# Raw weights and low parts in one buffer, seven weight homes, and a token tile at a time at the layer's seams

## The reference, cut to what matters

```python
h = layer_norm(x, ln_in_g, ln_in_b)
for i in range(DEPTH):                                   # DEPTH = 2, alpha = DN_ALPHA
    q, k, v, xr, yr, ga, gr = split(h @ w_in[i])         # 1024, 256, 256, then four of 1024 columns
    attn = local_attention(rope(q), rope(k), v, sink[i]) # 8 heads, window 128
    hr = rg_lru(conv(xr), forward) + rg_lru(conv(xr), backward)   # gates: two matmuls, then a scan
    rnn = hr * gelu(yr)
    merged = sigmoid(ga) * (attn @ w_proj_attn[i]) + sigmoid(gr) * (rnn @ w_proj_rnn[i])
    h = layer_norm(alpha * h + merged @ w_out[i], ln1_g[i], ln1_b[i])
    gate, val = split(h @ w_up[i])                       # 3072 columns each
    ffn = (gelu(conv3(gate)) * val) @ w_down[i]
    ple = sigmoid(h @ w_ple_gate[i]) * (p[i] @ w_ple[i])
    h = layer_norm(alpha * h + ffn + ple, ln2_g[i], ln2_b[i])
return h
```

## Time and profile before

| | us |
|---|---|
| median of 3 runs (985.03 to 986.15) | 985.28 |
| span of the profiled execution, first to last instruction | 984.2 |
| what lies around the span, by the median | about 1.1 |
| PE busy | 942.2 |
| DVE busy | 727.9 |
| ACT busy | 576.5 |
| DMA engines, mean share of the span | about a half |

### The profile page before, as it was taken

The page is one execution under the profiler, slowest core; times in us unless marked ns, Lnnn a source line. Parts: engine busy times, 40 slices in busy tenths (PEclk is TensorE's granted clock), DMA queues, the critical chain, the costliest instruction groups (busy, mean ns, idle before and its releaser), DMA issues.

```text
span 984.2 us, 12616 instructions
## 1 busy us (share of the span) xinstructions
PE 942.2 (96%) x5056; PEld 804.8 (82%) x5056; DVE 727.9 (74%) x974; ACT 576.5 (59%) x724; POOL 1.4 (0%) x9
## 2 busy tenths in 40 slices
PE   4999999999899999999979999999998999999995
PEld 2998889888678888888769888898886888888884
DVE  6879886777758676667777889877676776676658
ACT  3589988643356555546246999984335565455550
POOL 0000000000000000000000000000000000000000
PEclk9999999999999999999989999999999999999998
DMA  9464436384355656554725454455733755556541
GB/s 313 129 207 164 166 109 213 129 281 160 134 196 177 208 164 204 188 188 157 267 65 189 156 192 153 149 170 182 246 129 131 251 175 192 193 177 204 175 171 43
DMA packets 117753, 174.62 MB, mean 177 GB/s; under 512 B 3904, under 2 KB 78400, under 8 KB 117056
## 3 DMA queue, kind: packets, MB, share of 16 engines
q1 hardware_dynamic: 117408, 173.27, 52.6%
q10 hardware_dynamic: 288, 0.56, 0.1%
HBM read 172.76 MB, written 1.05 MB: 177 GB/s over the span
## 4 chain that ended last, share of the span: by engine, by line
PE 79%; DVE 14%; ACT 5%; issue 2%; DMA 1%; SPq 0%; DVEq 0%; ACTq 0%
PE ring L538 18%; PE ring L489 12%; PE ring L491 12%; PE ring L490 12%; PE ring L540 9%; DVE sb_w_lo L1089 4%; PE misc L489 4%; PE misc L491 4%; PE misc L490 4%; ACT sb_w_hi L787 2%; PE misc L637 2%; DVE sb_h L1139 1%; PE misc L695 1%; DVE sb_h L1136 1%; PE misc L675 1%
## 5 line engine op out<-in xcount | busy, mean ns | idle before, releaser
L1089 DVE TENSOR_TENSOR sb_w_lo<-sb_raw,sb_w_hi 128x2048 fp32r<-128x2048 f32 (+1 forms) x168 | 363.1, 2163 | 156.9 <-ACT sb_w_hi L787 156.6
L787 ACT CAST sb_w_hi<-sb_raw 128x2048 fp32r<-128x2048 f32 (+1 forms) x168 | 303.0, 1806 | 116.8 <-PE ring L491 73.6
L538 PE MATMUL ring<-sb_x_both,sb_w_hi 128*128 128x512 f32 x768 | 271.1, 398 | 3.3 <-DVE sb_w_lo L1089 3.3
L540 PE MATMUL ring<-sb_x_both,sb_w_lo 128*128 128x256 f32 x768 | 215.2, 280 | 0.0
L538 PEld LDWEIGHTS ring<-sb_x_both,sb_w_hi 128*128 128x128 f32 x768 | 144.2, 188 | 39.6 <-DVE sb_w_lo L1089 4.2
L489 PE MATMUL ring<-sb_w_hi,sb_x_both 128*128 128x512 f32 x352 | 142.5, 405 | 6.2 <-DVE sb_w_lo L1089 4.3
L540 PEld LDWEIGHTS ring<-sb_x_both,sb_w_lo 128*128 128x128 f32 x768 | 144.9, 189 | 0.3
L490 PE MATMUL ring<-sb_w_lo,sb_x_both 128*128 128x512 f32 x352 | 138.8, 394 | 0.0
L491 PE MATMUL ring<-sb_w_hi,sb_x_both 128*128 128x512 f32 x352 | 138.7, 394 | 0.0
L489 PEld LDWEIGHTS ring<-sb_w_hi,sb_x_both 128*128 128x128 f32 x352 | 67.3, 191 | 23.3 <-issue 4.4
L491 PEld LDWEIGHTS ring<-sb_w_hi,sb_x_both 128*128 128x128 f32 x352 | 67.0, 190 | 14.6
(11 more groups left out here) (140 smaller groups left out, 1335.1 us busy)
## 6 DMA issues: line engine op xcount, KB each, us to landing
sb_raw<-in_w_up_dram SPq DMA_DIRECT2D x48, 1024.0 KB, 5.2
sb_raw<-in_w_in_dram SPq DMA_DIRECT2D x44, 1024.0 KB, 5.2
sb_raw<-in_w_down_dram SPq DMA_DIRECT2D x24, 1024.0 KB, 5.0
sb_raw<-in_w_proj_attn_dram SPq DMA_DIRECT2D x8, 1024.0 KB, 5.0
sb_raw<-in_w_proj_rnn_dram SPq DMA_DIRECT2D x8, 1024.0 KB, 5.1
sb_raw<-in_w_out_dram SPq DMA_DIRECT2D x8, 1024.0 KB, 5.1
sb_raw<-in_w_ple_gate_dram SPq DMA_DIRECT2D x8, 1024.0 KB, 5.0
sb_lnp<-in_ln_dram SPq DMA_DIRECT2D x5, 1024.0 KB, 7.2
```

What stands on the lines that cost most here:

```text
L538: nc.tensor.matmul(bank_of(*key), w_hi[:, slot, cols], x_both[:, k], start=k == 0, stop=False)
L540: last = nc.tensor.matmul(bank_of(*key)[:, 0:SEQ], w_lo[:, slot, cols], x_hi[:, k], start=False, stop=k == KT - 1)
L787: nc.scalar.copy(w_hi[:, W_OF[n], 0:size], raw[:, slot, 0:size]).then_inc(s_hi_part, 1)
L1089: nc.vector.tensor_tensor(w_lo[:, W_OF[n], 0:size], raw[:, RAW_OF[n], 0:size], hi, ALU.subtract).then_inc(s_split, 1)
```

## The change

The source line numbers of the new kernel differ (cast L822, low part L1128, load L454, transposes L654, L1186 the add of the down product).

- **Homes.** `raw` and `w_lo` are now one buffer: DVE subtracts in place. There are five such homes with their `w_hi`, and two more that borrow other tensors while these are idle: `hb` with the scan's tensors (from `wo0` to the next layer's `q1`), and `r_lo`/`r_hi` (from `pg0` to the next layer's `q1`). A load now waits until PE has finished with the home's former item, since that item's low part lies there; the cast waits for the load alone. Homes go to the item in order of last use. `AHEAD` is 3, in places 4 or 5.
- **Output seam.** `wo0` and `wo1` run together, tile 0 through both, then tile 1, with the turns of tile 0 between the matmuls of tile 1; `pg0` tile 0, ple with the turns of tile 1, `pg0` tile 1. `pg1` follows here and no longer ahead of `d4`.
- **Layer seam.** `d4` and `d5` run together by tile; the first half of the next layer's tile 0 is turned inside tile 1 of `d5`; `q0` tile 0, one turn, a part of `q1` tile 0, the other turn, `q0` tile 1. `q1` moves from the second place in the mixer to here.
- **Mixer.** `WITH_BLOCK` loses `q1` and takes in `yr1`, and its order changes, so attention starts a block earlier. `yr0` is copied first and gets its gelu later.
- **Down products on DVE.** `add_ffn` adds the down product and takes the statistics half a tile at a time, and the high and low parts of `x_parts` go in between.
- **Embedding.** The two 128x2048 operations on DVE stand in groups j = 1 and j = 2 of the up units. `p_in` is loaded later, into `tmp`.

The core of the diff:

```diff
-BY_TILE = ("q0", "wo1", "pg0", f"d{LAST}")
-
-WITH_BLOCK = ("xr1", "q1", "kv", "ga0", "ga1", "gr0", "gr1", "yr0")
...
+WITH_BLOCK = ("xr1", "kv", "ga0", "ga1", "yr0", "gr0", "gr1", "yr1")
+
+
+def items_of():
+
+    items = [("q0", 0), ("q0", 1), ("q1", 0), ("q1", 1), ("xr0", 0), ("xr0", 1)]
+    for i, name in enumerate(WITH_BLOCK):
+        items += [(name, 0), (f"rg{i // RNN_BLOCKS}", i % RNN_BLOCKS), (name, 1)]
+    items += [(name, part) for name in ("pa0", "pa1", "pr0", "pr1") for part in range(2)]
+    items += [("wo0", 0), ("wo1", 0), ("wo0", 1), ("wo1", 1), ("pg0", 0), ("pg0", 1), ("ple", 0), ("ple", 1),
+              ("pg1", 0), ("pg1", 1)]
+    for j in range(FF_GROUPS):
+        names = [f"g{j}", f"v{j}"] + ([f"d{j - 1}"] if 0 < j < LAST else [])
+        items += [(name, part) for name in names for part in range(2)]
+    return items + [(f"d{j}", part) for j in (LAST - 1, LAST) for part in range(2)]
+
+
+ITEMS = [(l, name, part) for l in range(DEPTH) for name, part in items_of()]
 ITEM = {item: n for n, item in enumerate(ITEMS)}
-W_SLOTS = 3
-RAW_SLOTS = 3
-AHEAD = 2
+W_SLOTS = 5
+STATE_HOME, RNN_HOME = W_SLOTS, W_SLOTS + 1
+HOMES = W_SLOTS + 2
+AHEAD = 3
...
+def homes_of(n):
+
+    l, name, part = ITEMS[n]
+    at = n - ITEM[l, "q0", 0]
+    start, first, second = (ITEM[l, key, 0] - ITEM[l, "q0", 0] for key in ("xr0", "wo0", "pg0"))
+    homes = list(range(W_SLOTS))
+    if at < start or at >= first:
+        homes.append(STATE_HOME)
+    if at < start or at >= second:
+        homes.append(RNN_HOME)
+    return homes
+
+
+HOME, FORMER, LOADED = [], [], []
+_latest, _loads = {}, [0] * HOMES
+for _n, (_l, _name, _part) in enumerate(ITEMS):
+    _home = min(homes_of(_n), key=lambda home: _latest.get(home, home - HOMES))
+    _former = _latest.get(_home)
+    if _home >= W_SLOTS and _n > ITEM[_l, "xr0", 0] and (_former is None or _former < ITEM[_l, "xr0", 0]):
+        _former = "state" if _home == STATE_HOME else "rnn"
+    FORMER.append(_former)
+    HOME.append(_home)
+    _latest[_home] = _n
+    _loads[_home] += 16 * item_loads(_n)
+    LOADED.append(_loads[_home])
...
+        w_lo, at = sb_at("w_lo", [P, W_SLOTS, 2048], F32R)
+        raw = again("raw", [P, W_SLOTS, 2048], F32, at)
...
+        raw_at = [raw[:, i] for i in range(W_SLOTS)] + [whole(hb[:, :, :]), r_raw[:, :]]
+        hi_at = [w_hi[:, i] for i in range(W_SLOTS)] + [scan_hi[:, :], whole(r_hi[:, :, :])]
+        lo_at = [w_lo[:, i] for i in range(W_SLOTS)] + [hb_lo[:, :], whole(r_lo[:, :, :])]
...
+                former = FORMER[n]
+                if former == "state":
+                    sp.wait_ge(s_rnn_ready, value("rnn_ready", ITEMS[n][0], 2))
+                elif former == "rnn":
+                    sp.wait_ge(s_products, PRODUCT[ITEMS[n][0], "pr1", 1])
+                elif former is not None:
+                    sp.wait_ge(s_products, last_product(former))
+                home = HOME[n]
...
                 load_norm(l, 1)
-                for n in range(ITEM[l, "wo0", 1], ITEM[l, f"d{LAST}", 1] + 1):
+                sp.dma_start(p_in, a["p"][bass.ds(l, 1), 0].rearrange("a (t q) c -> q (a t) c", q=P)
+                             ).then_inc(s_p, 16)
+                for n in range(ITEM[l, "wo0", 0], ITEM[l, f"d{LAST}", 1] + 1):
...
+            def last_down_units(l):
+
                 for t in range(TT):
+                    for hh in range(2):
+                        if t == 0:
+                            pe.wait_ge(s_f_ready, value("f_ready", l, 2 * (LAST - 1) + hh + 1))
+                        part = down_part(l, LAST - 1, hh, t)
+                        if t == 1:
+                            part.then_inc(s_products, 1)
+                    if t == 1 and l + 1 < DEPTH:
+                        turn_h(l + 1, 0, 0, [0])
                     for c in range(2):
-                        first = down_part(l, j, 0, t, [c])
+                        if (t, c) == (0, 0):
+                            pe.wait_ge(s_f_ready, value("f_ready", l, 2 * LAST + 1))
+                        part = down_part(l, LAST, 0, t, [c])
                         if (t, c) == (1, 1):
-                            first.then_inc(s_products, 1)
-                        down_part(l, j, 1, t, [c]).then_inc(s_products, 1)
+                            part.then_inc(s_products, 1)
+                        if (t, c) == (0, 0):
+                            pe.wait_ge(s_f_ready, value("f_ready", l, 2 * LAST + 2))
+                        down_part(l, LAST, 1, t, [c]).then_inc(s_products, 1)
+                        if (t, c) == (1, 0) and l + 1 < DEPTH:
+                            turn_h(l + 1, 0, 0, [1])
...
+                token_part(l, "wo1", 0, 0, x)
+                x_ready(l, 4 + 4)
+                token_part(l, "wo0", 1, 0, x).then_inc(s_products, 1)
+                token_part(l, "wo1", 1, 0, x).then_inc(s_products, 1)
                 token_part(l, "wo0", 0, 1, x).then_inc(s_products, 1)
-                x_ready(l, 4 + 4)
-                token_half(l, "wo0", 1, x)
-                token_unit_by_tile(l, "wo1", x)
+                token_part(l, "wo1", 0, 1, x).then_inc(s_products, 1)
+                turn_h(l, 1, 0, [0])
+                token_part(l, "wo0", 1, 1, x).then_inc(s_products, 1)
+                turn_h(l, 1, 0, [1])
+                token_part(l, "wo1", 1, 1, x).then_inc(s_products, 1)
+                x_ready(l, 9)
+                token_part(l, "pg0", 0, 0, x)
+                x_ready(l, 10)
+                token_part(l, "pg0", 1, 0, x).then_inc(s_products, 1)
+                turn_h(l, 1, 1, [0])
                 ple_part(l, 0, 0)
-                turn_h(l, 1, 0)
                 ple_part(l, 0, 1)
-                token_unit_by_tile(l, "pg0", x, 8, after=lambda: pg0_tile_1(l))
+                turn_h(l, 1, 1, [1])
+                ple_part(l, 1, 0)
+                ple_part(l, 1, 1)
+                x_ready(l, 11)
+                token_part(l, "pg0", 0, 1, x).then_inc(s_products, 1)
+                x_ready(l, 12)
+                token_part(l, "pg0", 1, 1, x).then_inc(s_products, 1)
+                token_unit(l, "pg1", x)
...
+                home, size = HOME[n], item_size(n)
+                act.wait_ge(s_raw[home], LOADED[n])
+                nc.scalar.copy(hi_at[home][:, 0:size], raw_at[home][:, 0:size]).then_inc(s_hi_part, 1)
...
+                split_to(l, "pr0", 0)
+                split_to(l, "pr1", 0, 4)
                 x_parts(l, 4, [(0, 0), (1, 0)], 0.5)
-                split_to(l, "pr1", 1)
+                split_to(l, "pr1", 1, 4)
                 act.wait_ge(s_p_turned, value("p_turned", l, 1))
-                nc.scalar.activation(r_hi[:, 0:2, :].rearrange("p k s -> p (k s)"), misc[:, 1, :], ACT.Copy,
+                nc.scalar.activation(whole(a_hi[:, 0:2, :]), misc[:, 1, :], ACT.Copy,
                                      scale=1.0).then_inc(s_p_hi, 1)
-                split_to(l, "wo0", 0)
+                split_to(l, "pg0", 0, 0)
                 x_parts(l, 6, [(0, 1), (1, 1)], 0.5)
-                split_to(l, "wo1", 1)
-
-                x_parts(l, 8, [(0, 0), (0, 1)], 1.0)
-                split_to(l, "ple", 0)
+                split_to(l, "ple", 0, 0)
+                x_parts(l, 8, [(0, 0)], 1.0)
+                split_to(l, "ple", 1, 0)
+                x_parts(l, 9, [(0, 1)], 1.0)
+                split_to(l, "pg1", 0, 0)
```

539 lines of the change are left out of this document (249 added, 290 removed).

## The result

The changed kernel takes 974.48 us (median of 4 runs, 971.91 to 975.14) against 985.71 for the kernel before in the same comparison: a ratio of 0.9884 with an interval of [0.9872, 0.9896]. It is 11.2 us faster, where the sum had 15.4; the time lies inside the range (964 to 979), above the likeliest case's own (966.5 to 973). The profiled run took 974.05 with a span of 972.2.

A forecast was written before the change was run, and what follows sets the result against it. PE, busy 96% of the span, was taken as the bound, standing still mainly at seams and the end. Gains 9.3 + 2.5 + 0.8 + 1.8 + 1.0 = 15.4 us off the 984.2 span, plus 1.1, gave 969.9, said as 970; range 964 to 979.

The forecast's parts named there:

- likeliest case: Whole kernel: the terms hold as summed, 970 us, own range 966.5 to 973; chance 0.43.
- in the mixer they leave PE 0.5 us idle per layer, which the third item ahead covers: gain 1.0: Mixer, both layers: PE's idle time from waits for weights' low parts goes with more lead, gaining 1.0 us.
- Layer seam: Between layers: PE's work covers DVE's steps, 0.4 us of the 9.7 stays; gain 9.3 us, range 7.5 to 9.7.
- The new wait at the output seam: Output seam, each layer: PE waits 2.4 us behind ACT's cast, which waits for the load of pg0's first item.
- The 0.8 at tile 1's transposes: Output seam, each layer: PE waits 0.7 to 0.8 us because DVE does ple's half-size split before normalising.
- End of the program: After the last matmul: only the last half's add on DVE waits for PE and starts earlier; gain 1.8 us.
- The rival named the output seams: Output seams: the new waits bring on half clock, 1.6 us in each layer, 973 us; chance 0.15.
- The mixer becomes tight: Mixer: with q1 gone ACT has less idle time for in-order waits and PE loses time; mostly 973 to 979; chance 0.19.
- Loads come late everywhere: xr0 to pr1: PE waits at every item for loads; slower from 0.23 us per item, 1003 at 0.5; chance 0.06.
- The 7 us of room: Mixer: PE's four items take 16 to 19 us, load, cast and subtraction 9.2; some 7 us left for queueing.
- The head keeps its order: 0: Head of the program: its order stays the same, so no gain or cost.
- Embedding at cost 0: Up units: the embedding's 4.6 us on DVE hide under PE's 10.9 us down units; up to 4.6 per layer if uncovered.

The follow-up runs named there:

- experiment 4: Changed kernel with the two DVE operations that add the embedding moved back behind the last group of up units, just ahead of the layer seam: 979.52 us.
- experiment 5: Changed kernel with d4 again through both tiles before d5, and tile 0's transposes behind d5's tile 1: 977.76 us.
- experiment 2: Changed kernel with ACT's cast of pg0's first item moved behind the two high parts of the second merged half: 970.97 us.
- experiment 9: Kernel with rotation ahead of scan and cast behind high parts (966.1 us), plus DVE's split of ple's second item behind tile 1's normalising: 964.51 us.
- experiment 8: Kernel with rotation ahead of scan and cast behind high parts (966.10 us), with ACT's Sqrt in the recurrence replaced by Copy: 966.17 us.
- experiments 1 and 7: Each against the changed kernel: 1, DVE rotates q and k ahead of the first scan, 972.17 us; 7, PE turns them a tile later, 970.54 us.
- experiment 10: 964.5 us kernel (rotation ahead of scan, cast behind high parts, ple's split behind normalising), plus attention's steps ahead of the gate matrices' split: 963.39 us.
- Experiment 6: Changed kernel with four weight homes in the place of five (W_SLOTS = 4): 1010.37 us.

## Why the prediction was partly right

- **The number.** 974.5 is 4.5 us above the 970, and the misses behind it are larger, with both signs. By the profiled run, with the clock taken apart: mixers -3.0 us where +1.0 was said, new stretches of half clock -3.4 where nothing was said, head and up units -1.3 for 0; against these the layer seam 10.7 for 9.3, the output seams 4.1 and about 2.7 for 2.5 and 0.8, the end 2.0 for 1.8. That they partly cancel, and that layer 1's output seam shows 0.9 against 0.8, is luck. The time also lies in the tight mixer's 973 to 979.
- **The step that failed: "in the mixer they leave PE 0.5 us idle per layer, which the third item ahead covers: gain 1.0".** It asked only what the removed waits were worth. It didn't ask what else moves when q1 leaves `WITH_BLOCK`: the index of ga0, and with it what stands ahead of the rotation on DVE. The two blocks' rows could have been laid side by side before the run. The measured term is -4.6, of which 1.6 is the half clock behind the wait. "PE's idle time in the mixer not above 1 us" was wrong by 1.4.
- **Layer seam: right, a little small.** Full clock, and no wait in the list. By starts the embedding's place is worth 4.4 us of it (experiment 4) and the order by tiles with the transposes inside 2.3 (experiment 5); what makes the other 4 us of the 10.7 (the splits gone from DVE's way, the low parts between the adds, the former half clock) no run took apart. The term was 9.3: 0.4 was an allowance for waits that didn't come, and the stock of 9.7 was about 1 us small because it was read from the busy column of the earlier trace rows. A transpose there counts 0.60 to 0.66 us for four that start 0.11 apart. Starts tell it rightly. (The Trainium skill, "Perfetto Trace Analysis", section "Identifying the Most-Contended Engine", says that matmul busy time is not a good measure of how close a kernel is to its limit, because pipelined PE instructions look smaller in the trace. The trace agrees that the busy column is no measure; at these transposes they look longer, not smaller.) At layer 0's output seam (4.1 against 2.5) 2.7 us of waits were left and not 3.6, and the other 0.7 may be the same reading. This is read from the rows; no run isolated it.
- **The new wait at the output seam: right**, in place, cause and size (2.2 against 2.4); experiment 2 confirms it. **The 0.8 at tile 1's transposes: right** in place and cause, 0.5 to 0.65 in size; experiment 9.
- **End of the program: right** (2.0 against 1.8); experiment 5, without meaning to, shows that d4 and d5 by tile make it.
- **The clock.** The forecast took all 5.0 us of half clock at the seams as a gain, and they did go. But 3.4 us came back in two stretches elsewhere. The rival named the output seams; one of the two came there, in layer 1, and one in the mixer. I gave 0.15 to a thing that, by the mean clocks, the changed kernel did one to three times in each run, hardly less often than the kernel before (mean clocks 0.991 to 0.995).
- **"The mixer becomes tight" was the nearest rival**, with the wrong account: it summed up ACT's idle time, but experiment 8 takes 14 table loads from ACT without effect. Tight is the chain scores, softmax, mixed values through DVE and ACT; experiments 1 and 7 show that a 2.4 us wait taken away ahead of it comes back mostly as small ones, and experiment 10 that the order inside it decides.
- **"Loads come late everywhere"** is rejected for five homes. Experiment 6 shows that its account, the same delay at every item, is not how homes run out: they do so most at the units by tile. The 7 us of room was an average of the mixer, where a unit holds two homes, not four. (The stretch has 34 items per layer, not 33; the break-even of 0.23 us stays.)
- **"The head keeps its order: 0"** was right in order. The head took 0.5 us more, and full clock came later in it (at 21.5, before at 19.1); but kernels with this same head reached xr0 between 42.2 and 43.0 us (once at 44.7), against 31.2 + 10.9 = 42.1 before, so the 0.5 is within what one trace can differ from the next. **Embedding at cost 0**: no wait names it, and layer 1's up units take 179.3 us against 179.4 before. Layer 0's took 178.5 before and 179.3 now. The difference lies wholly in the first two groups, where the kernel before spaced 48 matmuls over 8.32 us and otherwise, like the changed kernel, over 8.48; why stays open, no run tried it.

## What to carry to other kernels

Where an order changes, print for each waiting engine what now stands ahead of every step that another engine waits for, also far from the place that the change is about; a rule by index ("every second block") moves with it. Size idle time from matmul starts between places of equal work, not from a busy column. A wait taken out of a chain of three engines that is as long as its cover was mostly handed on here: look at the chain's order before expecting its full size, and keep buffers enough for the unit that holds the most of them. Where a change moves pauses of a matrix engine about, list them by length as well as in sum: here half clock added 1.7 us to some of the waits of 2.1 to 2.4.
